# A decoder layer on one core: sample products padded to 128 partitions, and one joint low-part product in the prompt attention

## The chip, the cores and the metric

The kernel runs on one core of a Trainium2 chip. Its time is the device time of one execution in microseconds (us). Engines: TensorE (PE; its weight loads are shown apart, as PEld), VectorE (DVE), ScalarE (ACT), GpSimd (POOL), and SyncE (SP), which here only issues DMA transfers. TensorE's clock has two levels, 1.2 and 2.4 GHz; a granted clock of 1.00 is the upper one.

## What is computed

One layer of a decoder, for a prompt of 1024 tokens and for 8 samples of 4 tokens, with shared weights. After a norm and one wide projection come two branches: causal pooling over windows of 2 to 16 tokens, and sliding-window attention (16 query heads, 4 key/value heads, head size 64, window 128, with sinks). Both are gated and projected, and an output projection follows. The part that matters here:

```
s = q . k * HEAD_DIM**-0.5          # per head; rel = qpos - kpos
mask = (rel >= 0) & (rel <= WINDOW) & (kpos >= 0)
m = max(max(s), sink);  e = exp(s - m)
o = (e / (sum(e) + exp(sink - m))) . v
```

A prompt query sees the 128 keys before it and itself. A sample query sees the 128 cached keys of its sample, and the new keys of its own sample up to itself.

## The kernel before

Everything is float32 in and out. Large products run in a reduced float32 (F32R), with every operand cut into a high and a low part: x = hi + lo. A projection multiplies hi by hi, lo by hi and hi by lo (L684: 352 token columns each, three thirds of 1056 tokens), in tiles of 128 output columns by 1056 tokens and eight steps of 128 over the inner dimension. Nine products make a step.

**Prompt attention.** 8 blocks of 128 tokens by 4 key/value heads make 32 units. A unit is spread over four steps of the gate projection: `attention_half` hangs its pieces behind these steps, a list written out by hand. After step k0 the scores of the first 64 queries, after k0+1 those of the other 64 (`scores`, L933), after k0+2 the transposes of the unit before (L947, L951), after k0+3 that unit's product with the values (`values`, L964 and L968). A query tile `qt` holds on its 128 partitions the 64 high parts and below them the 64 low parts of a head; a key tile `kt` holds the high parts twice (in both halves of the partitions) and the low parts twice. So a score group is, for each of two pairs of heads, a product of the queries with the doubled high parts and one with the doubled low parts: four products of 192 keys. Two groups make a unit, 64 groups in all. These are the lines:

```python
for b in range(2):
    for part in range(2):
        keys = kt[:, kv, part, :, :].rearrange("p s n -> p (s n)")[:, k0:k0 + KW]
        last = nc.tensor.matmul(ps[:, bank, 256 * b:256 * b + KW],
                                qt[:, slot, s, 2 * b:2 * b + 2, :].rearrange("p g n -> p (g n)"), keys,
```

**Loads of the units.** Queries and keys are read back from `qk_d` in memory, values from `v_d`. All of these loads stand on SP's queue, in the order of the code. `load_unit` for unit u waits (L496) until the scores of unit u-2 are done, then issues unit u's queries and keys (`load_q_k`, L466 and L470) and after them the values of unit u-2 (`load_v`, L480 and L487, or L482 and L491 after the first block). Queries are 2 transfers of 128 KB in pieces of 256 bytes. Keys of a head stay in `kt` for two blocks: 4 transfers of 64 KB for an even block (m below 4), 2 for an odd one. Values are 3 transfers. In each eight units two weight chunks of 1 MB (L388, two transfers each) are issued as well, after the third and the seventh; GpSimd splits a chunk into its high and low part (L597, L599) when TensorE has freed the slot. The first eight units and the last eight are written out, the sixteen between are a loop of two turns with addresses from registers. The first load of unit 2 also waits until DVE has cleared the value tile (L1321), which comes after the first mask.

**Samples.** In four gate tiles before that, one key/value head at a time: transposes of cached keys, `sample_scores` (eight instructions at L868 for the cached keys, over 128 partitions, and two at L870 for the new keys, over the upper 64), softmax on DVE and ACT, transposes (L875, L876), then `sample_values` (two instructions at L885 for the new values over 32 partitions, and eight at L888 for the cached ones). A float32 product is two instructions. ACT copies the new keys and queries into `q_sum` (in `take_back`, into both halves), the new values into `v_group` (L1787), and the transposed probabilities into `spt` (L1790, L1791). In the last group DVE clears the unused third of the key tile (L1295) ahead of the scaling of a gate tile (L1285).

Of the kernel before, what the change touches and what calls it, by code (L numbers as in the profile page):

```python
# [187 lines left out]
def build(nc, xp, xs, cache_k, cache_v, state, pp, ps_, params, w_in, pool_map, w_pp, w_pa, w_out, w_ple,  # L188
          w_gate, const, masks, smask, y_p, y_s, nk_p, nv_p, npool_p, nk_s, nv_s, npool_s):
    with ExitStack() as ctx:  # L190
# [66 lines left out]
        with ExitStack() as s3:  # L257
            vt = sb("vt", [P, 2, 3, P], F32R, scope=s3)
            prob = sb("prob", [P, 2, 2, PW], scope=s3)
            gst = sb("gst", [P, 2, T], scope=s3)  # L260
            kt = sb("kt", [P, NKV, 2, 3, P], F32R, scope=s3)
            qt = sb("qt", [P, 2, 2, G, HD], F32R, scope=s3)
            msk = sb("msk", [P, 2, 2, KW], scope=s3)
            pt_hi, pt_lo, pt_edge = (sb(n, [P, G * P], F32R, scope=s3) for n in ("pt_hi", "pt_lo", "pt_edge"))
            st = sb("st", [P, 2, 6, G], scope=s3)
# [116 lines left out]
        def _(sp):  # L382
# [79 lines left out]
            def load_q_k(u, t, m):  # L462
                tok, kv = bass.ds(t * P, P), m % 4
                for a in range(2):
                    src = qk_d[G * kv:G * kv + G, :, bass.ds(t * P + HD * a, HD)]
                    sp.dma_start(qt[:, m % 2, a, :, :].bitcast(F32), src.rearrange("g p n -> p g n"))\  # L466
                        .then_inc(unit_loaded[kv], 16)
                for slot in ((2, 0) if m < 4 else (1,)):
                    for half in range(2):
                        sp.dma_start(kt[HD * half:HD * half + HD, kv, :, slot, :].bitcast(F32),  # L470
                                     qk_d[NH + kv, :, tok].rearrange("(s e) n -> e s n", s=2))\
                            .then_inc(unit_loaded[kv], 16)

# [28 lines left out]
            for h in range(2):  # L502
                sp.wait_ge(qk_stored[h], 16 * 10)
            for m in range(2):
                load_q_k(m, 0, m)
# [144 lines left out]
        def _(pe):  # L650
# [211 lines left out]
            def sample_scores(v):  # L862
# [4 lines left out]
                for p in range(NB // 2):  # L867
                    nc.tensor.matmul(ps[:, 7, 0:P], q_pair[:, P * p:P * p + P], kts[:, P * p:P * p + P],  # L868
                                     start=(p == 0), stop=(p == NB // 2 - 1))
                nc.tensor.matmul(ps[:, 7, P:SK], q_sum[0:HD, P * v:P * v + P], k_new[0:HD, NS * v:NS * v + NS],  # L870
                                 start=True, stop=True).then_inc(samp_done, 1)
# [10 lines left out]
            def sample_values(v, i, g):  # L882
                pe.wait_ge(spt_copied, v + 1)
                pe.wait_ge(vc_loaded[g], i * 16 + 16)
                nc.tensor.matmul(ps[:, 7, 0:P], v_group[0:NS].rearrange("p s e -> p (s e)"), spt[0:NS, 1, :],  # L885
                                 start=True, stop=False)
# [33 lines left out]

            def scores(u, m, i, s, first=False):
                slot, kv = m % 2, m % 4
                if first:
                    pe.wait_ge(samp_out, NKV + 1)
                    pe.wait_ge(zero_done, 1)
                if s == 0:
                    pe.wait_ge(unit_loaded[kv], i * 160 + (96 if m < 4 else 160))
                bank = round_of("S", u, s, m, first)
                k0 = (P if m < 4 else 0) + HD * s
                for b in range(2):  # L930
                    for part in range(2):
                        keys = kt[:, kv, part, :, :].rearrange("p s n -> p (s n)")[:, k0:k0 + KW]
                        last = nc.tensor.matmul(ps[:, bank, 256 * b:256 * b + KW],  # L933
                                                qt[:, slot, s, 2 * b:2 * b + 2, :].rearrange("p g n -> p (g n)"), keys,
                                                start=(part == 0), stop=(part == 1))
                last.then_inc(att_done, 1)
# [35 lines left out]
            def attention_half(i, m, k0, first):  # L972

                u, t = i * 8 + m, i * 2 + m // 4
                after, between = {k0: [], k0 + 1: [], k0 + 2: [], k0 + 3: []}, {}
                after[k0].append(lambda: scores(u, m, i, 0, first and m == 0))
                after[k0 + 1].append(lambda: scores(u, m, i, 1, first and m == 0))
                if not first or m >= 1:
# [151 lines left out]
        def _(dve):  # L1130
# [156 lines left out]
            def sample_group(kv, last_group=False):  # L1287
# [6 lines left out]
                if last_group:  # L1294
                    v.memset(kt[:, :, :, 1, :].bitcast(F32), 0.0).then_inc(zero_done, 1)  # L1295
                scale_za(kv, 0)
# [294 lines left out]
        def _(act):  # L1591
# [77 lines left out]
            def take_back(j, i):  # L1669
# [7 lines left out]
                if i == 2:  # L1677
                    for h in range(2):
                        col = NS * (q_head(j) + h)
                        for half in range(2):  # L1680
                            a.activation(q_sum[HD * half:HD * half + HD, col:col + NS],
                                         ps[HD * h:HD * h + HD, bank, 0:NS], ACT.Copy)
                a.activation(qkst[:, j % 2, 0, c0:c0 + w], ps[:, bank, 0:w], ACT.Copy).then_inc(back_hi, 1)

# [79 lines left out]
            with act.Fori(0, 2) as i:  # L1764
                for g in range(2):
# [18 lines left out]
                    for h in range(2):  # L1784
                        act.wait_ge(qk_stored[h], 16 * 10)
                    act.wait_ge(v_stored, 16 * 2)
                    a.activation(v_group[0:NS], kv_out[0:NS, 1, bass.ds(kv * HD + KV, HD)].unsqueeze(1)  # L1787
                                 .to_broadcast([NS, 2, HD]), ACT.Copy)
                    act.wait_ge(samp_done, kv * 4 + 3)
                    a.activation(spt[0:NS, 1, :], ps[0:NS, 6, P:2 * P], ACT.Copy)  # L1790
# [277 lines left out]
```

## Time and profile before

| | us |
|---|---|
| median of three runs | 1164.6 (1163.95 to 1164.92) |
| the profiled execution, its own time | 1165.1 |
| its span, first to last instruction | 1163.3 |
| TensorE busy | 1156.3 (99%) |
| DVE, ACT, GpSimd busy | 563.9, 395.9, 407.7 |
| granted TensorE clock, mean | 0.999 |

The rows of a profile name an instruction by line, engine and operation, then the tile written and the tiles read. `x4` is a count, the figures are start and length in us in a timeline, and total and mean elsewhere. A bracket at the end tells how long the engine idled before and what ended that. Busy times of products overlap, since they are pipelined; distances between starts are what a product costs. An engine's own instructions are followed by `q` where its sequencer acts, as for DMA issues (SPq).

### The profile page before, as it was taken

The numbers are of one execution on the slowest core, as the hardware profiler recorded it, in microseconds if no ns is written. First come the engines' busy times: TensorE is split into PE (matmuls) and PEld (weight loads), VectorE is DVE, ScalarE is ACT, GpSimd is POOL, SyncE is SP. The second block draws the span as 40 slices with busy tenths as digits, with TensorE's granted clock in tenths as the row PEclk, the third lists the DMA queues.
The fourth block names the chain that finished last, engine by engine and source line by source line (L and its number), as shares of the span: only waits on it lengthen the run. The fifth ranks groups of instructions, "written<-read, shape, count | busy, mean of one in ns | idle before, by whom it ended". The sixth has DMA issues, their size and how long they took to land.

```text
span 1163.3 us, 20002 instructions
## 1 busy us (share of the span) xinstructions
PE 1156.3 (99%) x7656; PEld 1143.1 (98%) x7656; DVE 563.9 (48%) x1045; ACT 395.9 (34%) x954; POOL 407.7 (35%) x191
## 2 busy tenths in 40 slices
PE   8999999999999999999999999999999999999998
PEld 8999999999999999999999999999999999999998
DVE  5566774112556566564726465832363451163322
ACT  6433334233766767666110010321321030031112
POOL 4433332333212222223333344335432532374310
PEclk9999999999999999999999999999999999999999
DMA  9425466313455555652611111072223232412211
GB/s 303 168 73 149 141 165 181 94 46 87 132 154 158 153 154 134 166 148 74 218 54 51 37 50 36 23 276 76 92 75 124 82 124 77 135 65 64 65 38 56
DMA packets 145791, 130.83 MB, mean 112 GB/s; under 512 B 49039, under 2 KB 134439, under 8 KB 145727
## 3 DMA queue, kind: packets, MB, share of 16 engines
q1 hardware_dynamic: 131063, 106.21, 30.0%
q10 hardware_dynamic: 14664, 23.74, 7.1%
q8 instruction: 44, 0.72, 0.2%
q14 instruction: 20, 0.16, 0.0%
HBM read 94.82 MB, written 37.12 MB: 113 GB/s over the span
## 4 chain that ended last, share of the span: by engine, by line
PE 99%; DMA 1%; SPq 0%; DVE 0%; issue 0%; DVEq 0%
PE ps L684 75%; PE ps L822 11%; PE ps L933 2%; PE ps L708 2%; PE ps L1092 1%; PE ps L964 1%; PE ps L947 1%; PE ps L784 1%; PE ps L698 1%; PE ps L968 1%; PE ps L951 1%; PE ps L1061 1%; DMA xr<-in_x_prompt 1%; PE ps L888 0%; PE ps L868 0%; PE ps L1040 0%
## 5 line engine op out<-in xcount | busy, mean ns | idle before, releaser
L684 PE MATMUL ps<-m_hi,w_hi 128*128 128x352 f32 x1704 | 556.1, 327 | 0.1
L684 PE MATMUL ps<-m_lo,w_hi 128*128 128x352 f32 x1704 | 548.1, 322 | 0.0
L684 PE MATMUL ps<-m_hi,w_lo 128*128 128x352 f32 x1704 | 369.8, 325 | 0.0
L684 PEld LDWEIGHTS ps<-m_hi,w_hi 128*128 128x128 f32 x1704 | 320.9, 188 | 1.3 <-issue 0.5
L684 PEld LDWEIGHTS ps<-m_lo,w_hi 128*128 128x128 f32 x1704 | 320.7, 188 | 0.0
L597 POOL TENSOR_TENSOR w_hi<-raw_a,w_one 128x1024 fp32r<-128x1024 f32 x41 | 78.9, 1923 | 683.4 <-PE ps L684 371.4
L684 PEld LDWEIGHTS ps<-m_hi,w_lo 128*128 128x128 f32 x1704 | 289.8, 188 | 0.0
L599 POOL TENSOR_TENSOR w_lo<-raw_b,w_hi 128x1024 fp32r<-128x1024 f32 x41 | 111.1, 2709 | 3.2
L599 POOL TENSOR_TENSOR w_lo<-raw_a,w_hi 128x1024 fp32r<-128x1024 f32 x41 | 104.1, 2539 | 3.2
L822 PE MATMUL ps<-w_lo,m_hi 128*128 128x256 f32 (+1 forms) x360 | 99.4, 282 | 0.0
L822 PE MATMUL ps<-w_hi,m_hi 128*128 128x256 f32 x320 | 92.3, 288 | 0.0
L597 POOL TENSOR_TENSOR w_hi<-raw_b,w_one 128x1024 fp32r<-128x1024 f32 x41 | 90.0, 2194 | 0.0
L822 PE MATMUL ps<-w_hi,m_lo 128*128 128x256 f32 x320 | 90.0, 281 | 0.0
L1937 ACT ACTIVATE gin<-gin 128x1056 f32<-128x1056 f32 x16 | 17.4, 1088 | 144.8 <-DVE gin L1480 144.8
L822 PEld LDWEIGHTS ps<-w_lo,m_hi 128*128 128x128 f32 (+1 forms) x360 | 64.5, 179 | 0.0
L822 PEld LDWEIGHTS ps<-w_hi,m_lo 128*128 128x128 f32 x320 | 60.5, 189 | 0.0
L822 PEld LDWEIGHTS ps<-w_hi,m_hi 128*128 128x128 f32 x320 | 60.2, 188 | 0.0
L1838 ACT ACTIVATE prob<-prob,st 128x193 f32<-128x193 f32 x128 | 56.5, 445 | 0.0
L1336 DVE CUSTOM_DVE_ANT_0 prob<-ps,msk,sinks_n 128x192 f32<-128x192 f32 x128 | 48.2, 417 | 6.1 <-issue 4.5
L1853 ACT ACTIVATE prob<-prob,st 128x192 f32<-128x192 f32 x128 | 47.5, 446 | 0.1
L1561 DVE TENSOR_TENSOR gin<-ps,rbc 128x1056 f32<-128x1056 f32 x7 | 8.8, 1258 | 70.1 <-PE ps L684 70.1
L1346 DVE TENSOR_TENSOR pt_lo<-ps,pt_hi 128x512 fp32r<-128x512 f32 x32 | 22.1, 692 | 42.4 <-ACT pt_hi L1815 42.4
(248 smaller groups left out, 1429.9 us busy)
## 6 DMA issues: line engine op xcount, KB each, us to landing
raw_a<-in_w_in SPq DMA_DIRECT2D x25, 512.0 KB, 3.7
raw_b<-in_w_in SPq DMA_DIRECT2D x25, 512.0 KB, 4.6
qk_d<-qkst ACTq DMA_DIRECT2D x20, 512.0 KB, 5.6
gate_d<-gst ACTq DMA_DIRECT2D x16, 528.0 KB, 3.4
gin<-gate_d SPq DMA_DIRECT2D x16, 528.0 KB, 3.6
qt<-qk_d SPq DMA_DIRECT2D x64, 128.0 KB, 3.5
kt<-qk_d SPq DMA_DIRECT2D x96, 64.0 KB, 2.5
vt<-v_d SPq DMA_DIRECT2D x84, 64.0 KB, 2.2
```

What stands on the lines that cost most here:

```text
L597: hi_count.did(nc.gpsimd.tensor_tensor(hi, raw[piece][:], one, ALU.mult))
L599: nc.gpsimd.tensor_tensor(lo, raw[piece][:], hi.bitcast(F32), ALU.subtract)\
L684: last = nc.tensor.matmul(ps[:, 3 * parity + c, 0:CH], w, x[:, k, CH * c:CH * c + CH], start=(k == 0 and w is wh and x is src_hi), stop=(k ...
L698: last = nc.tensor.transpose(ps[:, UNIT_BANK[i], at:at + P], xr[:, t, P * k:P * k + P], ident)
L708: return nc.tensor.matmul(ps[:, 3 * h + g, 0:n], wt[:, 0, k, P * h:P * h + P], x[:, k, c0:c0 + n], start=start, stop=(k == KT - 1 and x is ...
L822: last = nc.tensor.matmul(ps[0:m, block_bank(n), 0:WC], x, w, start=(k == 0 and a == 0), stop=(k == KT - 1 and a == len(parts) - 1))
L933: last = nc.tensor.matmul(ps[:, bank, 256 * b:256 * b + KW], qt[:, slot, s, 2 * b:2 * b + 2, :].rearrange("p g n -> p (g n)"), keys, start ...
L1336: last = v.tensor_tensor_reduce(prob[:, slot, b, seen_at(s):seen_at(s) + KW], ps[:, bank, 256 * b:256 * b + KW], msk[:, start, s, :], -1.0 ...
L1346: last = v.tensor_tensor(pt_lo[:], ps[:, bank, :], pt_hi[:].bitcast(F32), ALU.subtract)
L1838: last = a.activation(strip, strip, ACT.Exp, bias=st[:, slot, 0, g:g + 1], scale=-1.0, accum_out=st[:, slot, 3, g:g + 1])
L1853: last = a.activation(strip, strip, ACT.Copy, scale=st[:, slot, 5, g:g + 1])
L1937: a.activation(gin[:, h, :], gin[:, h, :], ACT.Sigmoid).then_inc(gate_opened, 1)
```

## The change

For new keys and new values of the samples, the operands are taken over all 128 partitions, with zeros below: `k_new`'s lower half, and the lower 96 partitions of `v_group` and of the second half of `spt`. In the prompt attention the low parts of the keys are multiplied with the high parts of the queries only, for both pairs of heads in one product: the stationary tile `q_high` holds the high parts of the heads of pair 0 on the upper 64 partitions and of pair 1 on the lower 64, and `kt` now has three planes, high parts twice, low parts above zeros, and zeros above low parts. The joint product streams the last two planes, 384 columns, into the two stretches of the bank, and starts their accumulation. The product of low part by low part is no longer computed. `kt` is now double-buffered by unit, and holds both blocks' keys of one head: each unit loads all that it sees, 256 tokens. A unit has 2 query transfers, 4 of `q_high` (32 KB, pieces of 256 bytes), 2 of keys, then the 3 of values.

```diff
-            kt = sb("kt", [P, NKV, 2, 3, P], F32R, scope=s3)
+            kt = sb("kt", [P, 2, 3, 2 * P], F32R, scope=s3)
+            k_gap = sb("k_gap", [P, 1024], scope=s3)
+            q_high = sb("q_high", [P, 2, 2, 2, HD], F32R, scope=s3)
@@ load_q_k
-                for slot in ((2, 0) if m < 4 else (1,)):
-                    for half in range(2):
-                        sp.dma_start(kt[HD * half:HD * half + HD, kv, :, slot, :].bitcast(F32),
-                                     qk_d[NH + kv, :, tok].rearrange("(s e) n -> e s n", s=2))\
-                            .then_inc(unit_loaded[kv], 16)
+                    for b in range(2):
+                        heads = qk_d[G * kv + 2 * b:G * kv + 2 * b + 2, 0:HD, bass.ds(t * P + HD * a, HD)]
+                        sp.dma_start(q_high[HD * b:HD * b + HD, m % 2, a, :, :].bitcast(F32),
+                                     heads.rearrange("g e n -> e g n")).then_inc(unit_loaded[kv], 16)
+                first = isinstance(t, int) and t == 0
+                seen = slice(0, P) if first else bass.ds(t * P - P, 2 * P)
+                for half in range(2):
+                    dst = kt[HD * half:HD * half + HD, m % 2, 0:2 + half:1 + half, P if first else 0:2 * P]
+                    sp.dma_start(dst.bitcast(F32), qk_d[NH + kv, :, seen].rearrange("(s e) n -> e s n", s=2))\
+                        .then_inc(unit_loaded[kv], 16)
@@ SP, before the first units' loads
+            sp.wait_ge(zero_done, 1)
@@ sample_scores, sample_values
-                nc.tensor.matmul(ps[:, 7, P:SK], q_sum[0:HD, P * v:P * v + P], k_new[0:HD, NS * v:NS * v + NS],
+                nc.tensor.matmul(ps[:, 7, P:SK], q_sum[:, P * v:P * v + P], k_new[:, NS * v:NS * v + NS],
-                nc.tensor.matmul(ps[:, 7, 0:P], v_group[0:NS].rearrange("p s e -> p (s e)"), spt[0:NS, 1, :],
+                nc.tensor.matmul(ps[:, 7, 0:P], v_group[:].rearrange("p s e -> p (s e)"), spt[:, 1, :],
@@ scores
-                    pe.wait_ge(unit_loaded[kv], i * 160 + (96 if m < 4 else 160))
+                    pe.wait_ge(unit_loaded[kv], t * 128 + 128)
-                k0 = (P if m < 4 else 0) + HD * s
+                seen = slice(HD * s, HD * s + KW)
+                nc.tensor.matmul(ps[:, bank, :].rearrange("p (b n) -> p b n", b=2)[:, :, 0:KW],
+                                 q_high[:, slot, s, :, :].rearrange("p g n -> p (g n)"), kt[:, slot, 1:3, seen],
+                                 start=True, stop=False)
                 for b in range(2):
-                    for part in range(2):
-                        keys = kt[:, kv, part, :, :].rearrange("p s n -> p (s n)")[:, k0:k0 + KW]
-                        last = nc.tensor.matmul(ps[:, bank, 256 * b:256 * b + KW],
-                                                qt[:, slot, s, 2 * b:2 * b + 2, :].rearrange("p g n -> p (g n)"), keys,
-                                                start=(part == 0), stop=(part == 1))
+                    last = nc.tensor.matmul(ps[:, bank, 256 * b:256 * b + KW],
+                                            qt[:, slot, s, 2 * b:2 * b + 2, :].rearrange("p g n -> p (g n)"),
+                                            kt[:, slot, 0, seen], start=False, stop=(b == 1))
@@ DVE, last sample group
-                    v.memset(kt[:, :, :, 1, :].bitcast(F32), 0.0).then_inc(zero_done, 1)
+                    v.memset(kt[:].bitcast(F32), 0.0).then_inc(zero_done, 1)
@@ ACT, take_back
-                        for half in range(2):
+                        for half in range(2 if j >= 2 else 1):
                             a.activation(q_sum[HD * half:HD * half + HD, col:col + NS],
                                          ps[HD * h:HD * h + HD, bank, 0:NS], ACT.Copy)
+                        if j < 2:
+                            a.memzero(q_sum[HD:P, col:col + NS])
@@ ACT, sample groups, ahead of L1790
+                    for rest in (slice(NS, HD), slice(HD, P)):
+                        a.memzero(v_group[rest])
+                        a.memzero(spt[rest, 1, :])
```

## Rows read from the trace of the kernel before

**Rows 1.** The page, the chain of work that ended last, by engine.
```profile
PE 99%; DMA 1%; SPq 0%; DVE 0%; issue 0%; DVEq 0%
```
**Rows 2.** Windows: stretch and its length, busy time (count) by engine, clock, DMA share, GB/s.
```profile
286.00:546.00 260.00, 259.94 (x1742) 254.25 (x1740) 153.72 (x544) 185.08 (x560) 71.07 (x35) 1.00 0.52 140
```
**Rows 3.** Timeline of TensorE's products around the first score group: start, length.
```profile
286.87 0.59 PE L933 MATMUL ps<-kt,qt 128*128 128x192 f32 x4
...
287.49 0.32 PE L684 MATMUL ps<-m_lo,w_hi 128*128 128x352 f32 x1
```
**Rows 4.** Timeline of the weight loads of the same group.
```profile
286.71 0.58 PEld L933 LDWEIGHTS ps<-kt,qt 128*128 128x128 f32 x4
287.21 0.19 PEld L684 LDWEIGHTS ps<-m_hi,w_hi 128*128 128x128 f32 x1
```
**Rows 5.** Timeline of TensorE in the first projection, products of 384 columns.
```profile
31.56 0.34 PE L708 MATMUL ps<-m_hi,w_hi 128*128 128x384 f32 x1
31.73 0.34 PE L708 MATMUL ps<-m_hi,w_lo 128*128 128x384 f32 x1
```
**Rows 6.** Timeline of the weight loads around the first group's new-key product.
```profile
188.67 1.02 PEld L868 LDWEIGHTS ps<-kts,q_pair 128*128 128x128 f32 x8
189.81 0.29 PEld L870 LDWEIGHTS ps<-q_sum 64*128 64x128 f32 x2
190.14 0.19 PEld L684 LDWEIGHTS ps<-m_hi,w_hi 128*128 128x128 f32 x1
```
**Rows 7.** Timeline of the weight loads around the first group's new-value product.
```profile
203.03 0.35 PEld L684 LDWEIGHTS ps<-m_hi,w_lo 128*128 128x128 f32 x2
203.61 0.29 PEld L885 LDWEIGHTS ps<-spt,v_group 32*128 32x128 f32 x2 [0.22 <-issue]
204.02 0.97 PEld L888 LDWEIGHTS ps<-spt,vc 128*128 128x128 f32 x8
```
**Rows 8.** Timelines of ACT (first and last group) and of DVE (last group).
```profile
199.36 0.27 ACT L1790 ACTIVATE spt<-ps 32x128 f32<-32x128 f32 x1 [0.74 <-PE ps L876]
...
279.75 0.27 ACT L1790 ACTIVATE spt<-ps 32x128 f32<-32x128 f32 x1 [2.27 <-PE ps L876]
...
271.39 0.91 DVE L1295 MEMSET kt<- 128x1024 f32 x1 [0.16 <-issue]
```
**Rows 9.** Waits of SP and GpSimd in 286 to 546: total us, times, longest.
```profile
SPq L466 <- PE ps L933: 61.6, 26, 3.9
...
POOL w_hi L597 <- PE ps L684: 205.7, 9, 23.8
```
**Rows 10.** Timeline of SP's queue, loads of units 2 and 3.
```profile
291.64 0.92 SPq L466 DMA_DIRECT2D qt<-qk_d  x2
...
295.21 0.60 SPq L480 DMA_DIRECT2D vt<-v_d  x1
...
298.31 1.05 SPq L466 DMA_DIRECT2D qt<-qk_d  x2
...
302.26 0.61 SPq L480 DMA_DIRECT2D vt<-v_d  x1
```
**Rows 11.** Timeline of TensorE, first product with the values of units 0 and 1.
```profile
299.47 0.40 PE L964 MATMUL ps<-pt_hi,vt 128*128 128x512 f32 x1
...
307.49 0.40 PE L964 MATMUL ps<-pt_hi,vt 128*128 128x512 f32 x1
```
**Rows 12.** Timeline of SP's queue, one unit of the loop with seven transfers.
```profile
441.34 0.94 SPq L466 DMA_DIRECT2D qt<-qk_d  x2
...
444.59 1.31 SPq L491 DMA_DIRECT2D vt<-v_d  x2
```
**Rows 13.** One line's instructions (ns min/median/max) and their landing, L487.
```profile
L487 SPq DMA_DIRECT2D vt<-v_d x8: 596/597/799, 295.9 to 315.7; - x8
...
DMA to landing us min/median/max: 2.0/2.3/2.9
```
**Rows 14.** Timeline of TensorE, the product with the values that rows 12 load.
```profile
452.61 0.40 PE L964 MATMUL ps<-pt_hi,vt 128*128 128x512 f32 x1
```

## The prediction before the run

> **What bounds the kernel now.** First the chain that ended last: nearly all of it is TensorE [rows 1]. The reader is to see that no other engine and no DMA holds a share worth an edit. Then the attention stage by a window: 260 us in which TensorE is busy 259.94 at a granted clock of 1.00 [rows 2]. So no product waits for data there, and only two kinds of edit can move the end: one that shortens TensorE's own sequence, or one that makes it wait. Third the timeline of TensorE and of its weight loads around the edited products, and last the SP queue, because the change puts more transfers on it.
>
> **Joint score product.** A score group is four products of 192 columns; there are 64 groups (32 units, two each). From the first score product at 286.87 to the second L684 product at 287.49 pass 0.62 us [rows 3]; one L684 product of 352 columns takes 0.16 (two loads of 0.19 that end 0.35 after the first began [rows 7]), so the group costs 0.46. The weight loads say why: four begin at 286.71 and the next, L684's, at 287.21 [rows 4]. The first is followed after 0.16, since it must let a 352-column product stream, and the other three 0.11 apart. 192 columns stream in less: 384 take 0.17 to 0.18 between starts [rows 5], so 192 take about 0.09, an estimate by halving. Each score product thus costs a slot of one weight load, 0.112, and streams for less.
>
> After the change the group is one product of 384 columns and two of 192. The columns are the same 768, the load slots one fewer. Costs: 0.175 (streaming now hides the second load) + 2 x 0.112 = 0.40 against 0.453 (0.62 less 0.16, with the third digit from 4 x 0.112), so 0.054 less per group, times 64 = **3.5 us less**. Low end: nothing, if writing two separated stretches of a bank makes the joint product dearer by that much. High end: a whole slot, 0.112 x 64 = 7.2, if the two short products hid behind the long one; two load slots remain, so I stay at 3.5.
>
> **Sample products.** There are four groups (kv 0 to 3), each with one product of new keys (64 rows) and one of new values (32 rows), two instructions each. In the new-key case the eight L868 loads run to 189.69, so the last began at 189.50 (a load lasts 0.19); L870's first begins at 189.81, 0.31 later instead of 0.11, and L684's first at 190.14, 0.22 after L870's second instead of 0.11 [rows 6]. With 128 rows I take L868's pitch throughout: 0.20 + 0.11 = 0.31 less. In the new-value case the last L684 load begins at 203.19, L885's first at 203.61 (0.42 where 0.16 is normal), and L888's first at 204.02 where L885's second began at about 203.72 (0.30, not 0.11) [rows 7]; less 0.05, because the second load then has to let a product stream, that is 0.39. Both, times four: **2.8 us less**. Low end nothing, high end 3.2; a loss is excluded, since eight full-height loads stand in the same rows at 0.11.
> The Trainium skill (TensorE: Matmul & The Clock Gate, LDWEIGHTS) speaks against this part: a load of 32 rows takes as long as one of 128, only columns count. By that rule the padding returns 0. The load's own duration does agree here (0.29 for two, 0.11 apart), but the distances on both sides of the pair do not, and I go by those.
>
> **Zeros for that.** ACT gets four clears per group before L1790, at 0.27 each (L1790's own) 1.1 us. It idles 0.74 before L1790 in the first group and 2.27 in the last [rows 8], so the first group's copies end 0.4 later, at about 200.2; TensorE asks for them at 203.2. Cost nothing, covered by 3 us. Clears in the query and key copies replace copies of the same size. The DVE clear of the key tile grows from 1024 to 1536 elements, 0.91 to 1.37 us [rows 8]; behind it on DVE stands the scaling of a gate tile, then a SiLU and the exponentials on ACT, 0.46 later; with the clears 1.6, inside the 2.27 of that last group. The new SP wait on that clear delays the first two units' loads by about 1 us: sixteen transfers at 0.65 from 272.8 have landed by 286; unit 0's eight by 280.5, wanted at 286.7, and unit 1's wanted at 293.4. Nothing again.
>
> **SP queue.** This is the part that can bite. Per unit SP issued 2 query, 4 or 2 key and 3 value transfers; now 2 query, 4 high-part query, 2 key, 3 value: 11 instead of 9 or 7, so 96 more in all. At 0.65 each (the four key loads and their kin in rows 10 advance by that) they are 62 us of SP time. SP's waits before the query loads, all for score products, are 61.6 us over 26 units [rows 9]: the cover exists and is just used up. What stands behind the new transfers is each unit's load of the values, which are due before the next scores' V product; the queries and keys themselves have over 4 us.
> - Start. Unit 2's loads begin at 291.64, held by the clear of the value tile; six transfers later, at 295.21, the values [rows 10]. With eight: 296.5; the third value load issues at 297.8 and lands 2.0 to 2.3 later [rows 13], 299.9 or so. The first V product runs at 299.47, its weights are loaded 0.16 before, and with the savings of two groups are wanted at 299.2 [rows 11]: a wait of 0.7. Unit 3's loads started at 298.31, now 1.3 later, 299.6; before, 3.95 to the values at 302.26, now 5.25, so 304.85; third one issued at 306.15; behind a weight chunk it lands up to 2.9 later [rows 13], 308.9; wanted at 307.33 - 0.2 + 0.7 = 307.8: a wait of 1.1. Unit 4 then starts at 306.8 and its values land by 315.9, wanted near 316.9. No third wait. **1.8 us more**, between 0.3 and 3.
> - Loop. A 7-transfer unit takes 4.7 us on SP (441.34 to 445.90 and the register steps) [rows 12]. Four more at 0.70 make 7.6. A unit of TensorE lasts 8.03 now (299.47 to 307.49, less the wait-free pitch savings 0.11 = 7.92). Eight units: 60.8 + 2 weight chunks at 1.2 + 0.6 of loop turn = 63.8 on SP against 63.4 on TensorE. SP falls behind at the units after a chunk. In that unit the last value load, now issued at 448.1 and landed 2.2 later, comes at 450.3 for a product that runs at 452.61 [rows 14]; these 2 us absorb it, save for single long issues. **0.8 us more**, 0 to 3.
> - No row shows a q_high load: 64 partitions, two 64-element pieces each. Nearest in shape is a value or key load over 64 partitions, 0.60 (L487) [rows 13], plus register steps; from below a query load at 0.4, from above the longest first-iteration L487, 0.80. I take 0.65 to 0.70. The weight chunks are issued up to 3 us later; GpSimd, which splits them, waits 205.7 us over 9 chunks in this stage, and for TensorE to free a slot, not for the chunk [rows 9]: nothing.
>
> The pieces of q_high are of 256 bytes, like those of the query loads. The Trainium skill (DMA: Bandwidth & Descriptors, Specifications) asks for at least 512 bytes, below which the DMA engine reads, modifies and writes; no run here shows that step, and the sum gives it nothing.
>
> **Sum.** -3.5 - 2.8 + 1.8 + 0.8 = -3.7 us. The profiled execution took 1165.1 (span 1163.3); the median of the three runs is 1164.6, 0.5 less. Put on the median: 1164.6 - 3.7 = 1160.9.
>
> **Rivals.**
> - No waits at all: q_high issues like a query load, 0.45; SP needs under 7 us per unit, the start costs at most 0.3. 1164.6 - 6.3 = 1158.3, or 1156 with part of the high end of the joint product. For it: query loads issue in 0.4; against: every 64-partition load in these rows takes 0.6. Chance 0.15.
> - SP becomes the bound, the side slower than before. Place: the V product's weight load, whose values are queued behind four q_high loads. If q_high costs 0.85, a unit takes 8.2 on SP, eight units 68.6 with chunks and turn against 63.4; over some 24 units 15 us, less 2 of cover and 2 in the last eight units, which have no register steps: 11. 1164.6 - 6.3 + 1.8 + 11 = 1171. It decides from 0.72 on; at 0.77 it has eaten the gain. For it: 62 us of issues against 62 of slack, and single issues of 0.80; against: the median of every row. Chance 0.17.
> - Little change, three ways: the joint product no cheaper (1164.4); the loop waits by 3 instead of 0.8 (1163.1); or padding worth nothing, 1164.6 - 3.5 + 2.6 = 1163.7. The last would be shown by the load starts around L870 and L885 staying 0.3 apart: the pairs would have to be slow for another reason than their height, such as the output's place; the skill's rule named above would have it so. It gets 0.06, the three together 0.18.
> - The forecast, 1159.2 to 1162.3: 0.50.
>
> **Numbers.** Under 0.2% (2.3 us) a measurement of this kernel can't tell from no change. Faster by more: forecast and the no-wait case, less a little for their edges, 0.64. Within: 0.19. Slower: 0.17. The range goes from 1157.5 (no waits, a little under) to 1168, into the SP case until no more than 2 in 10 lie outside.
>
> **What would show it.** In the changed kernel: L933's loads, three per group, and 0.56 from the first score product to the second L684 product; L870 and L885 loads 0.11 apart from their neighbours; TensorE idle before two early V products, near 299 and 308, released by value loads; SP's waits for score products down from 62 us to under 10. Wrong if the early waits are absent, if TensorE waits at V in the loop unit after unit (q_high dearer than 0.75), or if L870's loads keep their gaps.

## The result, and the profile after

The changed kernel takes 1172.3 us (median of five, 1169.3 to 1173.2) beside 1164.6 before: ratio 1.006, interval 1.0043 to 1.0076. That is slower by 0.6%, and outside the forecast range of 1157.5 to 1168. Its profiled execution took 1170.0 us, 4.9 more than the one of before.

The page of the changed kernel, the chain that ended last; before, TensorE held 99% of it [rows 1]:

```profile
PE 84%; SPq 12%; issue 2%; DMA 1%; DVE 0%; POOL 0%; ACT 0%; DVEq 0%; ACTq 0%; POOLq 0%
PE ps L692 64%; PE ps L830 11%; SPq L472 4%; SPq L478 2%; PE ps L716 2%; SPq L498 2%; SPq L468 2%; PE ps L1101 1%; DMA vt<-v_d 1%; PE ps L792 1%; SPq L489 1%; PE ps L973 1%; PE ps L1070 1%; DMA raw_a<-in_w_in 1%; PE ps L706 1%
```

SP's queue now holds 12%, and the lines under it are all of one unit's loads (L468 queries, L472 q_high, L478 keys, L489 and L498 values). 12% of the span of 1168.2 us is 140 us. A chain that runs for so long through issues of one queue means that these follow one another with nothing between them that they wait for. The waits of the attention stage say what TensorE waits for (us in total, times, longest):

```profile
PE ps L973 <- DMA vt<-v_d: 8.4, 9, 2.0
PEld ps L973 <- issue: 7.9, 5, 2.3
...
PE ps L973 <- DVE pt_edge L1362: 1.0, 1, 1.0
```

And those of SP's queue alone, from 286 to 546:

```profile
SPq L489 <- PE ps L942: 5.9, 1, 5.9
SPq L468 <- PE ps L942: 4.1, 5, 1.2
...
SPq L468 <- PE ps L956: 0.7, 2, 0.4
```

Ahead of the query loads SP waited 61.6 us for score products before [rows 9]; 4.1 are left (the 5.9 stand ahead of the last value loads, where it was 10.1, in two waits, before). In the loop, from 334.68 to 471.89, SP waits for nothing at all: it runs there at its own rate. TensorE was busy all through this stage [rows 2], and now waits in front of L973, the product with the values. One such place on TensorE's timeline:

```profile
303.76 0.64 PE L692 MATMUL ps<-m_hi,w_lo 128*128 128x352 f32 x3
304.82 0.47 PE L973 MATMUL ps<-pt_hi,vt 128*128 128x512 f32 x1 [0.42 <-DMA vt<-v_d]
```

**What became cheaper.** TensorE's timeline at the first score group answers to [rows 3]:

```profile
282.68 0.34 PE L938 MATMUL ps<-kt,q_high 128*128 128x384 f32 x1
282.86 0.36 PE L942 MATMUL ps<-kt,qt 128*128 128x192 f32 x2
...
283.24 0.32 PE L692 MATMUL ps<-m_lo,w_hi 128*128 128x352 f32 x1
```

From 282.68 to 283.24 pass 0.56 us where it was 0.62. And the weight loads around the sample products answer to [rows 6] and [rows 7]:

```profile
187.53 0.86 PEld L876 LDWEIGHTS ps<-kts,q_pair 128*128 128x128 f32 x7
188.31 0.30 PEld L878 LDWEIGHTS ps<-q_sum 128*128 128x128 f32 x2
188.54 0.19 PEld L692 LDWEIGHTS ps<-m_hi,w_hi 128*128 128x128 f32 x1
...
201.43 0.35 PEld L692 LDWEIGHTS ps<-m_hi,w_lo 128*128 128x128 f32 x2
201.76 0.35 PEld L893 LDWEIGHTS ps<-spt,v_group 128*128 128x128 f32 x2
202.02 0.97 PEld L896 LDWEIGHTS ps<-spt,vc 128*128 128x128 f32 x8
```

L878's pair begins 0.11 after the last L876 load (that one ended at 188.39, so it began at 188.20), and L692 follows L878's second load (188.42) after 0.12; at L893 the last L692 load began at 201.59, 0.17 ahead. The period of a sample group fell from 26.79 to 26.07 us.

**Where the time went.** The start of the first score product of units 0, 8, 24 and 31, from TensorE's timeline of every kernel, gives three stretches: first eight units, the two turns of the loop, the last eight. Two of these rows for each, before and then after:

```profile
349.81 0.47 PE L933 MATMUL ps<-kt,qt 128*128 128x192 f32 x3
...
479.14 0.48 PE L933 MATMUL ps<-kt,qt 128*128 128x192 f32 x3
```

```profile
347.60 0.34 PE L938 MATMUL ps<-kt,q_high 128*128 128x384 f32 x1
...
484.90 0.34 PE L938 MATMUL ps<-kt,q_high 128*128 128x384 f32 x1
```

The loop of 16 units takes 137.3 us instead of 129.3. All kernels side by side (us; "q" is the first score product of unit 0, the rest are stretches between units):

```
kernel                          q       0-8   8-24   24-31
before                          286.87  62.9  129.3  56.2
after                           282.68  64.9  137.3  55.5
samples alone                   284.40  63.0  129.3  56.3
joint product alone             287.25  65.6  137.0  55.5
q_high for two units only       282.89  62.2  127.7  55.5
q_high, four small loads        283.28  62.8  128.0  55.5
q_high, eight small loads       284.23  72.6  154.0  60.4
values first                    283.22  63.1  135.3  55.5
queries stored another way      314.91  62.1  127.7  55.5
values product at 64 rows       285.68  64.3  138.3  55.5
loop written out                283.29  65.7  127.7  55.6
written out, values first       283.26  62.5  127.7  55.5
```

Before has no waits there, and with the cheaper score group the wait-free stretches are 62.2, 127.7 and 55.5 (as in the kernel with q_high for two units only, which waits nowhere). So the changed kernel waits 2.7 us in the first eight units and 9.6 in the loop (the idle rows above hold 9.4 of these 12.3; the rest isn't recorded as idle ahead of a product). Against the profiled execution of before, by the stretches: -3.1 (joint product) -2.9 (samples) +2.7 +9.6 = 6.3. The stage ahead of the samples was 1.3 shorter in this execution, which leaves 5.0 for 4.9 measured; the run with the values product at 64 rows, the same kernel up to there, doesn't have these 1.3 (its first new-key product begins at 189.84, the changed kernel's at 188.42, the one of before at 189.81), so they are chance. The median lies 2.3 above the profiled run.

### The profile page after: what moved, and what is told of

Read it like the earlier page. It is cut to its first block, busy times and chain, and to the rows that moved or that the text cites. A ratio compares the mean times of both kernels' runs of the same rounds, so it can differ in the third digit from the quotient of the medians.

```text
span 1168.2 us, 20066 instructions
## 1 busy us (share of the span) xinstructions
PE 1151.4 (99%) x7592; PEld 1137.1 (97%) x7592; DVE 566.5 (48%) x1045; ACT 400.0 (34%) x970; POOL 409.3 (35%) x191
## 2 busy tenths in 40 slices
DMA packets 159616, 136.61 MB, mean 117 GB/s; under 512 B 66959, under 2 KB 148263, under 8 KB 159551
## 3 DMA queue, kind: packets, MB, share of 16 engines
q10 hardware_dynamic: 14664, 23.74, 6.7%
## 4 chain that ended last, share of the span: by engine, by line
PE 84%; SPq 12%; issue 2%; DMA 1%; DVE 0%; POOL 0%; ACT 0%; DVEq 0%; ACTq 0%; POOLq 0%
PE ps L692 64%; PE ps L830 11%; SPq L472 4%; SPq L478 2%; PE ps L716 2%; SPq L498 2%; SPq L468 2%; PE ps L1101 1%; DMA vt<-v_d 1%; PE ps L792 1%; SPq L489 1%; PE ps L973 1%; PE ps L1070 1%; DMA raw_a<-in_w_in 1%; PE ps L706 1%
## 5 line engine op out<-in xcount | busy, mean ns | idle before, releaser
L692 PE MATMUL ps<-m_hi,w_hi 128*128 128x352 f32 x1704 | 555.9, 327 | 0.0
L692 PE MATMUL ps<-m_lo,w_hi 128*128 128x352 f32 x1704 | 548.1, 322 | 0.0
L692 PE MATMUL ps<-m_hi,w_lo 128*128 128x352 f32 x1704 | 369.8, 325 | 0.0
L692 PEld LDWEIGHTS ps<-m_hi,w_hi 128*128 128x128 f32 x1704 | 321.0, 188 | 0.9 <-issue 0.2
L692 PEld LDWEIGHTS ps<-m_lo,w_hi 128*128 128x128 f32 x1704 | 320.7, 188 | 0.0
L692 PEld LDWEIGHTS ps<-m_hi,w_lo 128*128 128x128 f32 x1704 | 289.7, 188 | 0.0
L1829 ACT ACTIVATE pt_hi<-ps 128x512 fp32r<-128x512 f32 x32 | 19.1, 597 | 70.1 <-PE ps L956 70.1
## 6 DMA issues: line engine op xcount, KB each, us to landing
qt<-qk_d SPq DMA_DIRECT2D x64, 128.0 KB, 2.5
kt<-qk_d SPq DMA_DIRECT2D x56, 128.0 KB, 2.9
```

The costliest lines, as they stand in the source:

```text
L692: last = nc.tensor.matmul(ps[:, 3 * parity + c, 0:CH], w, x[:, k, CH * c:CH * c + CH], start=(k == 0 and w is wh and x is src_hi), stop=(k ...
```

## The experiments

**Two theories** after reading the traces. The queue: SP's own time per unit is over TensorE's, so the value loads, last in each unit, are issued late. The transfers: the loads are issued in time, and the added bytes and small pieces make them land late.

### Each half of the change alone

One kernel is the kernel before with the sample products at full height, the other the changed kernel with the old ones:

```diff
-ps[:, 7, P:SK], q_sum[0:HD, ...], k_new[0:HD, ...]
+ps[:, 7, P:SK], q_sum[:, ...], k_new[:, ...]
-ps[:, 7, 0:P], v_group[0:NS]..., spt[0:NS, 1, :]
+ps[:, 7, 0:P], v_group[:]..., spt[:, 1, :]
```

> The kernel before with the sample products over 128 partitions alone (zeros below, ACT's clears included), prompt attention as before. If the cost of the 64-row and 32-row products is the 0.3 us before and after them, four groups give 2.8 us: 1161.8, between 1161.2 and 1162.4. If the padding is worth nothing and the changed kernel's earlier start was chance: 1164.6.

> The changed kernel with the sample products as before. Both theories below put the whole loss into the prompt attention, so 2.8 us above the changed kernel: about 1175, at least 1172. If the loss had to do with the clears on ACT or the sample part, it would be under 1166.

Samples alone: 1162.7, ratio 0.9977 (0.9968 to 0.9987), 2.6 less against 2.8 worked out (the kernel before took 1165.2 in these runs; the range of the expectation had been set from 1164.6, and the time lies 0.3 above it). Joint product alone: 1174.4, ratio 1.008 (1.0063 to 1.0096). The whole slowdown is in the joint half, and the two halves add up: 1164.6 - 2.6 + 9.2 = 1171.2 for 1172.3 measured.

### q_high not loaded

After units 0 and 1, q_high isn't loaded. This leaves out the low-part scores of units 2 to 31 (stale values are used), at the same instructions on TensorE:

```diff
-                    for b in range(2):
+                    for b in range(2 if high else 0):
```

> The changed kernel, which loads q_high only for units 0 and 1; all later joint products use those stale high parts (so the low-part scores of units 2 to 31 are left out of the computation). Seven transfers per unit on SP. If the loads of q_high are the whole cost, by issue or by transfer, the two savings of TensorE are left: 1158.3 (1164.6 - 2.8 - 3.5), no wait at the products with the values. If the key loads of 256 tokens matter, or ACT and DVE run late by themselves: above 1161.

1158.3 (1158.2 to 1159.0), ratio 0.9946 (0.993 to 0.9963). TensorE waits nowhere in the stage, and SP has its slack back:

```profile
SPq L468 <- PE ps L942: 77.0, 28, 4.1
```

So both gains are there in full (6.9 us under its own runs of before, 1165.2, for 6.3 worked out), and the q_high loads cost 14.0 us on the median. It also clears two terms: the clears on ACT and DVE, which the forecast had put at nothing, and the key loads of 256 tokens. This doesn't yet tell issue from transfer.

### Small loads: four, then eight

Four q_high loads per unit as before, but of 16 rows and one head, 4 KB instead of 32; then eight such loads, a quarter of the full bytes. Both leave out most of q_high after the first two units:

```diff
+                        ne, ng = (HD, 2) if high else (16, 1)
-                        heads = qk_d[...:G * kv + 2 * b + 2, 0:HD, ...]
+                        heads = qk_d[...:G * kv + 2 * b + ng, 0:ne, ...]
```

> The changed kernel; from unit 2 on each of the four q_high loads of a unit moves 16 rows of 256 bytes (4 KB) in place of 128 rows (32 KB), so most of q_high is stale. As many issues on SP's queue, an eighth of the bytes. Queue theory (the number of issues, about 0.65 to 0.8 us each, is the cost): 1169 to 1173 as the changed kernel, TensorE waiting at the products with the values in the loop. Transfer theory (the 256-byte pieces load the DMA engines and values land late): 1158 to 1161.

1160.2 (1159.9 to 1161.1), ratio 0.9961 (0.9947 to 0.9975). The queue's expectation, as I had put it, missed: I had counted transfers. The trace says what I had left out. The q_high line of this kernel and then of the changed kernel (duration of the issue in ns, minimum, median, maximum):

```profile
L473 SPq DMA_DIRECT2D q_high<-qk_d x128: 315/451/1774, 270.3 to 519.1; - x128
```

```profile
L472 SPq DMA_DIRECT2D q_high<-qk_d x128: 595/607/1816, 269.7 to 531.1; - x128
```

A small transfer is issued in less time, 0.16 less, 0.6 for a unit's four; that is just enough, SP waits for score products again (15.9 us, 17 times). So this run fits both theories, and eight small loads tell them apart: few bytes, much issue.

> As e4, but with eight small loads of q_high per unit instead of four (16 rows of 256 bytes each, most of q_high stale), 15 transfers per unit on SP and still a quarter of the bytes of the changed kernel. Queue theory: at the 0.45 us of a small issue in e4 plus register steps a unit takes some 1.6 to 2.1 us longer on SP than in e4, where it just fitted: 30 units put TensorE 35 to 60 us behind: 1195 to 1220. Transfer theory: the bytes are few, 1158 to 1163.

1200.8 us (one run). A quarter of the bytes, and by far the longest loop, 154.0. The granted clock was 0.94 from 357 to 511, the loop; that didn't set the length, since SP hardly waited for TensorE there. Waits of TensorE and of SP, and the q_high line:

```profile
PE ps L976 <- DMA vt<-v_d: 25.3, 18, 3.1
...
SPq L468 <- PE ps L959: 1.2, 2, 1.0
```

```profile
L475 SPq DMA_DIRECT2D q_high<-qk_d x248: 315/420/1337, 271.2 to 563.1; - x124
```

The transfer theory, which had 1158 to 1163, falls, as far as it goes by bytes; the queue's 1195 to 1220 holds. The landings say the same. The last value loads of a unit land in the changed kernel about as they did before:

```profile
L498 SPq DMA_DIRECT2D vt<-v_d x56: 595/607/936, 323.6 to 543.8; - x56
DMA to landing us min/median/max: 2.2/2.3/4.5
```

Before (L491) it was 2.2/2.2/3.6. Single slow landings of up to 4.5 us decide at which unit a wait falls, but not how long the loop is, for SP waits for nothing in it. What counts is the time that SP spends per unit.

### Values ahead of queries and keys

```diff
-                load_q_k(u, t, m)
                 load_v(2 * i + (m - 2) // 4, (m - 2) % 8)
+                load_q_k(u, t, m)
```

> The changed kernel with the loads of the values issued ahead of the queries and keys in each unit; same transfers, same products. If the loss is only the order (values queued behind q_high are due first), it goes: 1159 to 1161. If SP's queue is short of throughput (8.6 us of issues per unit in the loop against 7.9 of TensorE), the lateness collects as before and meets the queries and keys instead, which have some 3 us more room: 1168 to 1170, with TensorE waiting at the score products.

1167.6 (1166.5 to 1169.6), ratio 1.0025 (1.0015 to 1.0034), just under the 1168 to 1170 of the queue and far from the 1159 to 1161 of the order. Most of the wait at the start is gone (63.1 for 64.9), but only 2.0 us of the loop's (135.3 for 137.3): the wait is at the scores now.

```profile
PE ps L938 <- DMA kt<-qk_d: 5.5, 7, 1.8
```

Order helps where SP is late for once, not where it is late in every unit.

### Queries stored another way

Queries go to memory by pair and half block, so that a unit needs one query load and two q_high loads, eight transfers in all with the same bytes; the stores, on ACT's queue, are four per pair with 256-byte pieces instead of two:

```diff
-    qk_d[q_head(j) + h, :, 0:SEQ].rearrange("(s e) n -> e s n", s=2)
+    q_d[j - 2, HD * s:HD * s + HD, :].rearrange("e (c h n) -> e c h n", h=2, n=HD)[:, :, h]
```

> The changed kernel with the queries stored in memory by pair of heads and half block, so that one transfer brings all queries of a unit and two bring q_high, in pieces of 1 KB: eight transfers per unit (1 + 2 + 2 + 3) for the same bytes as the changed kernel. The stores of the queries on ACT's queue become four per pair instead of two, in pieces of 256 bytes. Queue theory: a unit takes under 6 us on SP, no waits at the values: 1158.3, up to 1160 if the stores cost something in the projection. Transfer theory: the same 640 KB per unit, so the loss stays in part: 1163 or more.

1193.2 (1190.0 to 1197.2), ratio 1.0249 (1.0234 to 1.0265). The expectation for the whole missed, though the attention stage did what it said: 62.1, 127.7 and 55.5 with the full bytes of queries and q_high, no wait. The loss is ahead of it: unit 0 starts at 314.91, 32 us later. TensorE there waits for the slot of the stores' staging tile; under that wait stands the page's line on ACT's queue:

```profile
PE ps L793 <- DVE qkst L1223: 22.4, 3, 7.6
```

```profile
q10 hardware_dynamic: 45640, 23.74, 7.9%
```

ACT's queue q10 moved the same 23.74 MB in 45640 packets, 14664 in the changed kernel. The granted clock fell as well, to a mean of 0.90 from 100 to 200 us (1.00 in the changed kernel); a tenth of 100 us is 10, by estimate what is missing from 22.4 to 32. In the attention stage, then, the same bytes land in time with fewer issues. This is a second sign against bytes as the cause, but not against small pieces: the query loads have pieces of 1 KB here, and the loads' queue q1 moved its 111.97 MB in 106487 packets where the changed kernel needed 144887.

### New-value product at 64 rows

The samples' gaps could come from a small row count or from any change of it:

```diff
-v_group[:].rearrange("p s e -> p (s e)"), spt[:, 1, :]
+v_group[0:HD].rearrange("p s e -> p (s e)"), spt[0:HD, 1, :]
```

> The changed kernel with the new-value product over 64 partitions instead of 128 (the new keys stay at 128). If only the height counts that a weight load shares with its neighbours, the load of L893 starts late by the 0.25 us of before and L896's by 0.19, as with 32 rows, and each of the four groups is 0.39 longer than in the changed kernel. If 64 rows are enough to be free of it, the distances are 0.16 and 0.11.

1173.4 us (one run), which by itself can't be told from the changed kernel's 1172.3. The period of a sample group can: 26.47 us for 26.07, 0.40 more, where 0.39 was expected. The load rows:

```profile
202.85 0.35 PEld L692 LDWEIGHTS ps<-m_hi,w_lo 128*128 128x128 f32 x2
203.43 0.29 PEld L893 LDWEIGHTS ps<-spt,v_group 64*128 64x128 f32 x2 [0.22 <-issue]
203.84 0.41 PEld L896 LDWEIGHTS ps<-spt,vc 128*128 128x128 f32 x3
```

The last L692 load began at 203.02; 0.41 to L893's first, then 0.30 from its second (203.54) to L896's first: the gaps of 32 rows [rows 7]. So 64 rows cost here what 32 did.

### The loop written out

SP's loop of units 8 to 23 uses a register for the addresses. Written out, every address is a constant, and the transfers are the same (159616 packets and 136.61 MB in the pages of both kernels); the second kernel also loads the values first:

```diff
-            with sp.Fori(1, 3) as i:
+            for i in range(1, 3):
```

> The changed kernel with SP's loop over units 8 to 23 written out, so that addresses are constants and no register steps stand between the transfers; same eleven transfers in the same order. Queue theory with the issue time as the cost: the distance of two transfers falls from 0.7 to 0.8 us to 0.65, a unit from 8.15 to about 7.2 on SP, under TensorE's 7.93, so the waits of the loop (9.7 us in the changed kernel) go and those of the first eight units (2.8) stay: 1160.5 to 1162. If it is the number of transfers or their bytes whatever an issue takes: no better than 1168.

> As e9, and in each unit the values ahead of the queries and keys. The first eight units' waits were at the values of units 0 and 1 and once behind a weight chunk; the queries and keys have 3 us more room. Queue theory: no wait left, 1158.3, up to 1159.5. This is the candidate for a version ahead of both kernels. If order alone had been what mattered, e6 would have shown it and this adds nothing to e9.

Written out: 1162.0 (1160.8 to 1163.6), ratio 0.9976 (0.9965 to 0.9986). With the values first: 1159.2 (1158.2 to 1162.4), ratio 0.9958 (0.9945 to 0.9972). The loop's waits are gone in both (127.7). The first eight units of the first one take 65.7, 3.5 of them waits where 2.8 were expected to stay; a pair of q_high issues there takes 3.41 us (from 327.50). With bytes, pieces, number and order of the transfers unchanged, only SP's time between and in the issues is left as the cause of the loop's 9.6 us. The reason stands in SP's timeline of one unit, first the changed kernel, then the written-out one:

```profile
446.71 0.38 SPq L468 DMA_DIRECT2D qt<-qk_d  x1
447.19 1.40 SPq L472 DMA_DIRECT2D q_high<-qk_d  x2
448.77 0.46 SPq L468 DMA_DIRECT2D qt<-qk_d  x1
449.32 1.40 SPq L472 DMA_DIRECT2D q_high<-qk_d  x2
450.90 1.29 SPq L478 DMA_DIRECT2D kt<-qk_d  x2
452.38 0.45 SPq L489 DMA_DIRECT2D vt<-v_d  x1
453.01 1.30 SPq L498 DMA_DIRECT2D vt<-v_d  x2
454.61 0.60 SPq L468 DMA_DIRECT2D qt<-qk_d  x1
```

```profile
407.32 0.60 SPq L468 DMA_DIRECT2D qt<-qk_d  x1
407.96 1.22 SPq L472 DMA_DIRECT2D q_high<-qk_d  x2
409.23 0.60 SPq L468 DMA_DIRECT2D qt<-qk_d  x1
409.86 1.22 SPq L472 DMA_DIRECT2D q_high<-qk_d  x2
...
412.43 0.59 SPq L489 DMA_DIRECT2D vt<-v_d  x1
413.06 1.22 SPq L498 DMA_DIRECT2D vt<-v_d  x2
```

446.71 to 454.61, where the next unit begins, is 7.9 us; 407.32 to 414.28, where the last issue ends and SP waits again, is 7.0. The loop's second query load and its first value load are even issued faster (0.46 and 0.45 for 0.60), but a pair of q_high loads and what leads to the next transfer takes 1.58 us (447.19 to 448.77) for 1.27 (407.96 to 409.23). In the loop register instructions stand between the issues, and written out there are none. These are the ones of the q_high line in the changed kernel:

```profile
L472 SPq MOVE q_high<-qk_d x64: 29/29/38, 335.1 to 467.3; - x64
L472 SPq FUSED_REGOPS  x32: 37/42/47, 336.1 to 467.2; - x32
```

For 64 issues of the loop they make 0.05 us each; the distance between two such loads is longer by 0.15, and no view shows the rest. The 0.9 us of a unit lie on one side and on the other of TensorE's period of 127.7 / 16 = 7.98 once chunks, the turn and long issues are added: SP's mean unit in the loop is then 8.6 (137.2 / 16, worked out below), and written out it stays under the period. With the loop written out SP waits for score products again:

```profile
SPq L468 <- PE ps L942: 11.7, 14, 1.5
```

In the last kernel TensorE holds 99% of the chain, as before. It beats both kernels, by 5.4 us (0.4%) the kernel before.

## Why the prediction was wrong

**Right: the joint product.** 0.56 us for the group, as worked out; the last stretch, which has no waits before or after, fell from 56.2 to 55.5, and 14 groups at 0.054 are 0.76. Over the 62 groups of the three stretches it is 3.1 for 3.3. Writing two separated stretches of a bank made nothing dearer.

**Right: the sample products.** 26.79 to 26.07 is 0.72 per group against 0.70, and 2.6 us measured alone. The run at 64 rows bears out the reading: the load's own duration stays (two in 0.29), the distances to its neighbours don't. The Trainium skill (TensorE: Matmul & The Clock Gate, LDWEIGHTS) says that the height costs nothing, which holds for the load by itself and would have given 0 here. The Trainium skill (TensorEngine Tiling (Array Packing), Key Properties) has it that a switch of tile mode requires a drain; the gaps of 0.2 to 0.3 us on each side agree with that, and it states no price. Whether it is a drain no run here shows.

**Right: what was costed at nothing.** The clears on ACT and DVE: with q_high not loaded the kernel has them all and the full 6.3 us of gain. The later issue of the weight chunks, which that kernel doesn't have: in the changed kernel GpSimd waits 173.4 us for TensorE to free a slot (286 to 546), and never for a chunk.

**Nearly right: the start.** 2.7 us of waits in the first eight units, for 1.8 in the sum and 3 at the bound. Two of them stand at the first two V products as forecast (idle 0.98 and 0.42 us in the records). The first of them is put down to DVE's pt_edge, but it goes with the order of the loads: values first takes the stretch to 63.1, and to 62.5 with the loop written out. "No third wait" failed, for there is one, at the unit after a weight chunk, where a pair of q_high issues had taken 2.47 us (from 328.58):

```profile
337.43 0.47 PE L973 MATMUL ps<-pt_hi,vt 128*128 128x512 f32 x1 [0.61 <-DMA vt<-v_d]
```

**Wrong: the loop, "0.8 us more".** It was 9.6. The forecast had 16 units at 7.6, four chunks at 1.2 and two turns at 0.6: 127.6 us on SP. In the trace of the changed kernel SP needs 137.2 for them (334.68 to 471.89). The four chunks advance it by 1.24 each (as from 360.02 to 361.26) and the turn between by 0.4, which leaves 8.24 per unit. So the term that was mis-sized is the unit, "Four more at 0.70 make 7.6", and two things are in it.

The first is the price of a transfer in the loop. The seven other transfers take 4.74 us of the undisturbed unit (7.90 less 4 x 0.79), as forecast (4.7). The issue of q_high was taken nearly rightly, 0.607 in the median, but 0.09 short with the register steps: it advances SP by 0.79 on average (1.58 for two), not by 0.70. That makes 7.9 (4.7 and 2.8 are 7.5, where the forecast wrote 7.6). The price could have been read in the trace of before, in the very unit of [rows 12]: two key loads over 64 partitions advance SP by 1.50, 0.75 each.

```profile
442.46 1.31 SPq L470 DMA_DIRECT2D kt<-qk_d  x2
443.96 0.45 SPq L482 DMA_DIRECT2D vt<-v_d  x1
```

The second is what the forecast put at nothing with "save for single long issues". They add the other 0.34 to the mean unit, as here in the keys, 2.11 where 1.29 is usual; TensorE's wait for the values of that unit follows:

```profile
363.89 1.39 SPq L472 DMA_DIRECT2D q_high<-qk_d  x2
365.46 2.11 SPq L478 DMA_DIRECT2D kt<-qk_d  x2
```

```profile
371.89 0.47 PE L973 MATMUL ps<-pt_hi,vt 128*128 128x512 f32 x1 [2.04 <-DMA vt<-v_d]
```

0.30 and 0.34 per unit, times 16, and 0.2 for the chunks are 10.4; the turn was 0.8 cheaper than two at 0.6. That is the whole miss of 9.6. The next sentence of the forecast failed with it, "these 2 us absorb it". They can, if a queue is late after a chunk and catches up. This one, at 137 for 127.7, never does, and lateness is carried into the next unit; the 2 us are used up once. The forecast had 63.8 against 63.4 on its own numbers, so the sum stood on the edge: 4% on the unit, 7.9 for 7.6, already puts SP some 4 us over TensorE's 127.7.

**The rival was the right one.** "SP becomes the bound" (1171, chance 0.17) named the place, the way and nearly the time, and its condition held: it was to decide from 0.72 per q_high load, register steps in it, and the load advanced SP by 0.79. The sign "q_high dearer than 0.75" held too. That the time came so near is partly luck. The rival had a unit at 8.2 from loads at 0.85; the mean unit was 8.24, from loads at 0.79 and long issues that were in no sum.

**Left open.** What makes single issues take 1 to 2 us: they come with and without a weight chunk ahead, and the loop's first turn has more of them (8.4 us per unit on SP, 8.1 in the second). Why a changed row count holds up its neighbours. Moving the q_high loads to another engine's queue wasn't tried.

## What to carry to other kernels

A queue that issues transfers is an engine with a budget: add up, per period of the bound engine, the distance from start to start of its issues in the very loop in question, register steps and chunks in it, and set the sum against the period. Here, under the period, four extra transfers a unit cost little (128.0 for 127.7 with small loads); over it, TensorE was late by the whole difference (137.2 on SP less 127.7 is 9.5, and it waited 9.6), and another order brought back 2.0 of it. An undisturbed unit of 7.90 against a period of 7.98 was already over, since chunks and single long issues made it 8.6 in the mean (137.2 / 16, turn included). So with a sum within some 5% of the period, count the queue as the bound, and look for cheaper addresses (a loop written out) ahead of fewer bytes.

## What the hardware showed unexpectedly

- The issue time of a transfer on SP's queue depends on its shape: 0.45 us in the median for 16 rows of 64 elements, 0.61 for 64 rows of two pieces.
- A register in the address costs SP 0.9 us in a unit of eleven transfers, most of it behind the q_high loads (0.79 from start to start for 0.64), of which the register instructions in the trace make 0.05.
- Stores of the same bytes in 256-byte pieces (45640 packets for 14664) started unit 0 some 32 us later, 22.4 of it TensorE's waits for the staging tile that these stores read. The q_high loads have pieces of 256 bytes too, and beside them the value loads landed after 2.3 us in the median (2.2 before).
- The weight loads of a product over 64 or 32 rows last no longer among loads of 128 rows, but they and the ones behind them start late. This cost 0.40 us a group for the new-value product at 64 rows and 0.32 for the new-key one (26.79 less 26.47).
- In two kernels in which TensorE waited often, the granted clock fell below 1.00: 0.94 in the mean of the loop with eight small loads (357 to 511 us), 0.90 from 100 to 200 us with the queries stored another way. In the mean of the span the others have 0.998 to 1.000.
